# Dense attention stage: values as high and low part become the weights of the weighting, turned probabilities are streamed in two parts, the result is turned at the end

## The reference

```
def dense_block_attention(q, k, v):        # q: (B, L, Hkv, G, Dh); k, v: (B, L, Hkv, Dh)
    ...
        s = einsum('bqhgd,bkhd->bhgqk', qi, k) * scale      # scale = Dh ** -0.5
        p = softmax(s, axis=-1)
        return einsum('bhgqk,bkhd->bqhgd', p, v)
...
    qb = rms_norm(qb.reshape(b, l, B_KV_HEADS, g_b, HEAD_DIM), qn_b)
    kb = rms_norm(kb.reshape(b, l, B_KV_HEADS, HEAD_DIM), kn_b)
...
    ob = dense_block_attention(axial(qb), axial(kb), vb)    # axial: rotation of both halves of a head
```

## Time and profile before

| | us |
|---|---|
| median of 3 runs | 3950.07 |
| the profiled execution | 3949.25 |
| its span | 3947.4 |
| PE busy (matmul) | 3802.8 (96%) |
| PEld busy | 3570.8 (90%) |
| DVE busy | 2643.0 (67%) |
| ACT busy | 2096.3 (53%) |
| POOL busy | 854.5 (22%) |

### The profile page before, as it was taken

One profiled execution on the slowest core, in us unless ns is written; L12 is line 12 of the kernel. 1 busy time (PEld: TensorE's weight loads), 2 busy tenths in 40 slices (PEclk: granted clock), 3 DMA queues, 4 the chain that ended last, 5 costly groups with the idle time before them and its releaser, 6 DMA issues. The chain is left out here.

```text
span 3947.4 us, 70746 instructions
## 1 busy us (share of the span) xinstructions
PE 3802.8 (96%) x24950; PEld 3570.8 (90%) x24950; DVE 2643.0 (67%) x5354; ACT 2096.3 (53%) x3837; POOL 854.5 (22%) x1367
## 2 busy tenths in 40 slices
PE   8999999999999889999999999999997999999998
PEld 7989989999987789999999989999886999999998
DVE  6565664676665677777777757777536777777775
ACT  6544554555552255565556556555323556655654
POOL 5132230333330011121111133323000111111112
PEclk9999999999999999999999999999898999999999
DMA  3000001122124378887788731000335788778874
GB/s 110 10 22 7 24 17 36 45 69 64 49 97 154 130 248 248 264 256 241 243 266 255 242 91 47 31 24 16 137 139 192 234 251 271 246 238 252 270 245 134
DMA packets 492025, 583.96 MB, mean 148 GB/s; under 512 B 21536, under 2 KB 447520, under 8 KB 491808
## 3 DMA queue, kind: packets, MB, share of 16 engines
q1 hardware_dynamic: 473952, 522.44, 41.1%
q0 software_dynamic: 15680, 50.34, 5.4%
q10 hardware_dynamic: 2176, 8.39, 0.5%
HBM read 514.89 MB, written 66.22 MB: 147 GB/s over the span
## 5 line engine op out<-in xcount | busy, mean ns | idle before, releaser
L1774 DVE TENSOR_TENSOR wl<-raw,wh 128x2048 fp32r<-128x2048 f32 x384 | 876.1, 2289 | 193.6 <-ACT wh L1717 175.0
L1717 ACT CAST wh<-raw 128x2048 fp32r<-128x2048 f32 x384 | 730.5, 1910 | 24.4 <-DMA raw<-in_w_gate 22.1
L1890 PE MATMUL ps_g<-xT,wh 128*128 128x384 f32 x2048 | 594.2, 356 | 0.3 <-DVE xT L1780 0.3
L1890 PE MATMUL ps_u<-xT,wh 128*128 128x384 f32 x2048 | 593.5, 356 | 0.0
L1892 PE MATMUL ps_g<-xT,wl 128*128 128x192 f32 x2048 | 477.5, 254 | 0.0
L1892 PE MATMUL ps_u<-xT,wl 128*128 128x192 f32 x2048 | 477.3, 254 | 0.0
L151 PE MATMUL psP<-ring_high,hTh 128*128 128x384 f32 (+1 forms) x1344 | 459.8, 342 | 12.5 <-DVE ring_low L826 6.3
L153 PE MATMUL psP<-ring_high,hTl 128*128 128x384 f32 (+1 forms) x1344 | 441.3, 328 | 0.0
L152 PE MATMUL psP<-ring_low,hTh 128*128 128x384 f32 (+1 forms) x1344 | 440.9, 328 | 0.0
L1080 PEld LDWEIGHTS psO<-V,pT 128*128 128x128 f32 x3456 | 421.4, 194 | 20.3 <-issue 10.2
L1080 PE MATMUL psO<-V,pT 128*128 128x64 f32 x3456 | 419.5, 274 | 4.9 <-ACT pT L759 3.0
(11 more groups left out here) (219 smaller groups left out, 7715.4 us busy)
## 6 DMA issues: line engine op xcount, KB each, us to landing
raw<-in_w_gate SPq DMA_DIRECT2D x128, 1024.0 KB, 5.7
raw<-in_w_up SPq DMA_DIRECT2D x128, 1024.0 KB, 5.8
raw<-in_w_down SPq DMA_DIRECT2D x128, 1024.0 KB, 8.3
xb<-in_x SPq DMA_DIRECT2D x72, 256.0 KB, 2.8
out_y<-yb SPq DMA_DIRECT2D x24, 512.0 KB, 2.6
h_rows<-hb SPq DMA_DIRECT2D x24, 512.0 KB, 3.0
ring_raw<-in_w_a SPq DMA_DIRECT2D x24, 384.0 KB, 3.8
xb<-in_x SPq DMA_DIRECT2D x12, 512.0 KB, 4.6
```

The lines of the kernel that those rows point to most:

```text
L1717: act.copy(wh[:, j % SPL], raw[:, j % RAW]).then_inc(w_high, 1)
L1774: dve.tensor_tensor(wl[:, j % SPL], raw[:, j % RAW], wh[:, j % SPL].bitcast(F32), ALU.subtract)\
L1890: both = lambda **fl: pe.matmul(ps[:, f, 0:2 * CAP], wh[:, j % SPL, k, fs], xT[:, k].rearrange("p h c -> p (h c)"), **fl)
```

## The change

All of it is in the dense stage.

- The values are kept as a high part (fp32r) and a low part, side by side in `V` (128 columns). ACT writes them twice, once in float32 to `v32` and once rounded to `V`; POOL subtracts (the low part).
- Turned probabilities too: ACT copies both batches rounded (the high part), DVE subtracts from PSUM (the low part). `pT` has three places instead of two.
- For each block of keys one fp32r product: the weights are the 128 columns of `V`, and 256 columns are streamed, 128 of the high and 128 of the low part of the turned probabilities. In PSUM stand then four parts, turned around (features by queries): two halves of columns and two halves of rows.
- DVE adds the halves of columns (`join`, into `oT`), PE turns the sum (`turn_output`, event "O"), DVE adds the two other halves into `osb` (`add_halves`), and ACT divides (`divide`).
- The weighting of a unit is cut in two: its second batch comes after the transposes of the next unit. The list is R(n), V(n - 1, 1), S(n + 2), O(n - 1), V(n, 0).
- On DVE the maximum of unit n + 2 moves behind the additions of unit n - 1, and gives the negative maximum at once; the factor `SCALE` goes into the gains. The rotation's first product moves from DVE to POOL (four products per tile, into `xr`, after `squared`). In the unit after a projection `rotate` and `scale` now stand right behind the second subtraction (the event V(n - 1, 1) calls `tile_up_to(3)`), ahead of `add_halves` and of the maximum.
- To make room, x has three places instead of four, inside `qT`, and the rotation table holds each distinct part once, loaded by four transfers instead of one.

The diff, cut to its core:

```diff
@@ -351,12 +351,15 @@
                 events.append(("T", turned))
 
         for kind, n in plan:
+            if kind == "U" and n:
+                events += [("R", n), ("V", n - 1, 1)]
+            elif kind == "U":
+                events.append(("R", n))
             if kind == "P":
                 turn_up_to(n - 2)
...
                     since[p] += 1
-                events.append(("V", n))
+                if n:
+                    events.append(("O", n - 1))
+                events.append(("V", n, 0))
             else:
...
+    if dense:
+
+        x_places = [nc.alloc_sbuf_tensor_at(f"xb{x}_{state['n']}", [P, HC], F32, offset=qT_at + 4 * (x * TOK + TOK - HC))
+                    for x in range(XH)]
     kT = ph.sb("kT", [P, nkv, 2, TOK], F32R)
-    V = ph.sb("V", [P, NT, nkv * HD])
+    V = ph.sb("V", [P, NT, 2 * HD], F32R) if dense else ph.sb("V", [P, NT, nkv * HD])
     prob = ph.sb("prob", [P, 2, 2 * KC])
-    pT = ph.sb("pT", [P, 2, BLK * P]) if dense else ph.sb("pT", [P, nq // 2, 2 * KC])
+    if dense:
+        pT = ph.sb("pT", [P, SLOTS, BLK, 2, P], F32R)
+        v32 = ph.sb("v32", [P, 2, HD])
+        oT = ph.sb("oT", [P, 2, 2 * P])
+    else:
...
+                if dense:
+                    pool.tensor_tensor(V[:, t, HD:], v32[:, b, :], V[:, t, 0:HD].bitcast(F32), ALU.subtract).then_inc(v_split, 1)
                 for a in range(S1):
...
-                                                 spread(sn[:, c0:c0 + R1], 1, nh), ALU.mult)
+                        sn = rope[:, NT if a else t, (1 + f) * R1:(2 + f) * R1] if dense else rope[:, s, t, 1, c0:c0 + R1]
+                        ins = pool.tensor_tensor(qx[:, b, :, c0:c0 + R1], x[:, :, c1:c1 + R1], spread(sn, 1, nh), ALU.mult)
+                if dense:
+                    wait_alone(pool, squared, p + 1, tally)
+                    turned_x = xr[:, b, :].rearrange("p (h c) -> p h c", c=HD)
+                    for c0 in range(0, HD, R1):
+                        cs = rope[:, NT if c0 >= 2 * R1 else t, 0:R1]
+                        ins = pool.tensor_tensor(turned_x[:, :, c0:c0 + R1], x[:, :, c0:c0 + R1], spread(cs, 1, nh), ALU.mult)
                 ins.then_inc(crossed, 1)
                 wait_alone(pool, summed, p + 1, tally)
                 chain.link(pool.tensor_scalar(ms[:, b, :], ss[:, b, :], 1.0 / HD, em[:, steps[s]["order"], t:t + 1],
...
                 act.copy(xr[:, b, :], psP[:, 0:nh * HD])
-                act.mul(V[:, t, :], psP[:, nh * HD:NC], rt[:, steps[s]["order"], t:t + 1]).then_inc(evacuated, 1)
+                if dense:
+                    if p >= 2:
+                        act.wait_ge(v_split, p - 1)
+                    act.mul(v32[:, b, :], psP[:, nh * HD:NC], rt[:, 0, t:t + 1])
+                act.mul(V[:, t, 0:nkv * HD], psP[:, nh * HD:NC], rt[:, steps[s]["order"], t:t + 1]).then_inc(evacuated, 1)
 
             def square(p):
...
-                act.copy(pT[:, slot, at:at + w], room_of("R", u, k)[:, 0:w]).then_inc(pT_act, 1)
+                if dense:
+                    act.copy(pT[:, slot, :, 0, :], room_of("R", u, k).rearrange("p (x c) -> p x c", c=P)).then_inc(pT_act, 1)
+                else:
...
+            def divide(u):
+
+                segs = units[u][1]
+                act.wait_ge(rden_ready, u + 1)
+                act.wait_ge(o_added, u + 1)
+                for c, (h, t, *_) in enumerate(segs):
+                    out = osb[:, (units[u][0] * NT + t) % OR, h]
+                    ins = act.mul(out, out, rden[:, u % 4, c:c + 1])
+                ins.then_inc(o_done, 1)
 
...
+            def turned_low(u, k):
+                slot = work.spot(u, k)[0]
+                dve.wait_ge(pT_act, batch0[u] + k + 1)
+                dve.tensor_tensor(pT[:, slot, :, 1, :], room_of("R", u, k).rearrange("p (x c) -> p x c", c=P),
+                                  pT[:, slot, :, 0, :].bitcast(F32), ALU.subtract).then_inc(pT_dve, 1)
+
+            def join(u):
+
+                segs = units[u][1]
+                dve.wait_ge(pv_done, batch0[u] + 2)
...
+                for c in range(len(segs)):
+                    ins = dve.tensor_reduce(oT[:, u % 2, c * P:(c + 1) * P], o_half(u, c).rearrange("p (f c) -> p c f", f=2),
+                                            AX.X, ALU.add)
+                ins.then_inc(o_summed, 1)
+
+            def add_halves(u):
+
+                i, segs = units[u][0:2]
+                ns, (h, t) = len(segs), segs[0][0:2]
...
+                dve.wait_ge(exp_done, u + 1)
+                dve.reciprocal(rden[:, u % 4, 0:ns], den[:, u % 4, 0:ns]).then_inc(rden_ready, 1)
+                p = i * NT + t
+                if h == 0:
+                    for x in range(p, p + ns):
+                        if x >= OR:
...
+                dve.tensor_reduce(osb[:, p % OR:p % OR + ns, h],
+                                  room_of("O", u)[:, 0:ns * P].rearrange("p (n f c) -> p n c f", f=2, c=HD),
+                                  AX.X, ALU.add).then_inc(o_added, 1)
+
+            waiting = []
+
+            def maxima():
...
                     x_low_part(e[1], e[2])
-                if e[0] == "R":
+                if e[0] == "R" and dense:
+                    turned_low(e[1], 0)
+                    if e[1]:
+                        join(e[1] - 1)
+                    turned_low(e[1], 1)
+                    tile_up_to(1)
+                elif e[0] == "R":
                     copies(e[1])
-                    if dense:
-                        tile_up_to(1)
-                if e[0] == "S":
+                if e[0] == "S" and dense and e[1] > 1:
+                    waiting.append(e[1])
+                elif e[0] == "S":
                     if e[1] == 0:
                         mask_constants()
                     maximum(e[1])
-                    if dense:
-                        tile_up_to(2)
+                if e[0] == "O":
+                    if e[1] == UT - 1:
+                        join(e[1])
+                    add_halves(e[1])
+                    tile_up_to(2)
...
-                if e[0] == "V":
+                if e[0] == "V" and dense:
+                    maxima()
+                    tile_up_to(3)
+                elif e[0] == "V":
                     output(e[1])
-                    if dense:
-                        tile_up_to(3)
                 if e[0] == "OL":
...
 
+            def weigh_batch(u, k):
+                segs = units[u][1]
+                if k == 0:
+                    both = u > 0 and max(len(segs), len(units[u - 1][1])) > 1
+                    if u - 1 + both > 0:
+                        pe.wait_ge(o_summed, u - 1 + both)
+                    pe.wait_ge(v_split, units[u][3] + 1)
+                copied(u, k)
+                slot = work.spot(u, k)[0]
+                for x, (c, j) in enumerate(units[u][2][k]):
+                    k0, nk = segs[c][2:4]
+                    ins = pe.matmul(o_half(u, c), V[:, k0 + j, :], pT[:, slot, x, :, :].rearrange("p f c -> p (f c)"),
+                                    start=(j == 0), stop=(j == nk - 1))
+                ins.then_inc(pv_done, 1)
+
+            def turn_output(u):
+                pe.wait_ge(o_summed, u + 1)
+                room_free(("O", u))
+                for c in range(len(units[u][1])):
+                    ins = pe.transpose(room_of("O", u)[:, c * P:(c + 1) * P], oT[:, u % 2, c * P:(c + 1) * P], ident)
+                ins.then_inc(o_turned, 1)
+
             idle_bank = psS[:, 0, 0:P]
             if fresh[0]:
```

118 lines of the change are left out of this document (79 added, 39 removed).

## The result

The changed kernel takes 4052.66 us (median of 4 runs, 4049.59 to 4060.3) where the kernel before takes 3949.70: 103 us more, ratio 1.0267 with a 95% interval of 1.0255 to 1.0279. The direction was forecast, the size was not: 57 us were expected, and the time lies 8 us above the top of the range. The profiled execution of the changed kernel, the longest of its four, has a span of 4058.5 us, that of before 3947.4.

A forecast was written before the change was run, and what follows sets the result against it. TensorE bounds the unit before; after, three engines share one tight loop (2.87, 3.00, 3.04 us). Terms -48 + 56 + 9 + 19 + 11 + 9 + 1.4 = +57.4 on 3950.07 give 4007.5 us, range 3940 to 4045.

The forecast's parts named there:

- The unit: Sample units of the dense stage: 3.04 us each instead of 3.54, over 96 units -48 us.
- rival D: Much slower: the sum of halves runs at half rate, 0.35 us a unit more; 4041 us, chance 0.12.
- Rival B: Faster: TensorE stays the bound, waits at tiles covered but for 1 us; 3917 us, chance 0.15.
- A projection between units: Twelve places where a projection stands between units: 9.03 us over three units against 4.38, +56 us.
- (1): After the projection ScalarE empties PSUM before copying probabilities: first copy at +1.47 instead of +0.65, subtraction at +2.11.
- (2): VectorE's rotation and scaling, waiting for GpSimd, precede sum and maximum: a step of 6.3 us where a unit has 3.04.
- step (3): Next unit's second transposes wait for that sum, then weighting, scores, tile's turn and low parts follow: a step of 4.55.
- The stretches: Stretches of projections: GpSimd's longer chain at two pairs of tiles a turn, 3 us in each of three turns, +9.
- The start: Start of the dense stage: three places for x and GpSimd's 6.4 us a tile against 5.6, +9 us together.
- Passages and quarters: Four places where a stretch passes into units, +19 us; low parts of ten weight quarters no longer hidden, +11 us.
- What was to show it: Signs: maximum every 3.0 to 3.1 us, 18 us over three steps, VectorE idle over 2 us a tile, stage past 700.
- C: Even: units gain 64 us as with TensorE the bound, but 3 us are lost per tile; 3949 us, chance 0.12.

The follow-up runs named there:

- e4: Changed kernel with one of GpSimd's four cosine products a tile, the other three left out; 4011.61 us.
- f1: Changed kernel with all of a tile's cosine products on VectorE (two instructions) instead of GpSimd (four); 4012.91 us.
- f3: Changed kernel with later rotation and scaling, a later turn for tiles between units, and cosine products on VectorE; 3991.05 us.
- g1: Changed kernel with that later order, cosine products on GpSimd for tiles projected between units and on VectorE for the others; 3977.38 us.

## Why the prediction was wrong

**The unit: right.** 3.05 us against 3.04 forecast; prompt units 3.53 against 3.5. The two subtractions take 685 ns, the sum of halves 415 ns: the row of 416 ns with plain order was the right one to take, and rival D, the sum at half rate, is out. The other units gained 22.7 us where 30 less 2 for the quarters stood, 28: eight of the 62 steps are prompt units, which gained nothing. Rival B, TensorE stays the bound, is out too: TensorE is idle 153 of 776 us. The judgement by the share of weight loads, for which the prediction named the Trainium skill, "Perfetto Trace Analysis", Identifying the Most-Contended Engine, pointed to TensorE before; the changed trace shows what it can't see, that the engine with 407 of 672 us was next and had its slack in the wrong places.

**A projection between units: the mechanism right, 24 us too little.** Steps (1), (2) and (3) gave 18.15 us for three steps; with the clock held up they are 18.22, in the changed kernel 19.6 to 20.4 (20.7 to 21.1 at the first place of a turn). What failed is that step (3) was worked out with durations of a TensorE at 2.4 GHz, behind a wait of its own making. The second long step is 4.5 us at 1.00 and 5.7 to 6.4 with the clock down: 19.5 us over 12 places. In the earlier trace rows the clock is 1.00, and TensorE's longest idle stretch between two products of that stage is 1.9 us; a forecast that makes it idle has to ask what the next products then cost. The other 5 us are mostly the first places of three turns, where the first step is 11.9 us instead of 10.7: it holds the sums of a prompt unit and two weight quarters that the prediction's ten don't include.

**The stretches: mis-sized, +9 against +31.8.** The prediction counted GpSimd's longer chain for two pairs of tiles in a turn's stretch, 1.5 us each. Timeline of the changed kernel in one:

```profile
436.36 0.32 ACT L760 ACTIVATE V<-psP,roots 128x64 fp32r<-128x64 f32 x1
...
437.77 0.32 POOL L694 TENSOR_TENSOR V<-v,V 128x64 fp32r<-128x64 f32 x1
...
439.17 1.16 POOL L705 TENSOR_TENSOR xr<-xg,rope 128x64 f32<-128x64 f32 x4
440.37 0.43 DVE L921 TENSOR_TENSOR xg<-xr,qx 128x256 f32<-128x256 f32 x1 [2.78 <-POOL xr L705]
...
442.11 0.82 DVE L929 TENSOR_TENSOR xn<-xg,rstd 128x192 f32<-128x192 f32 x1 [1.31 <-POOL rstd L710]
442.85 0.34 DVE L933 TENSOR_SCALAR xn<-xg,rstd 128x128 f32<-128x128 f32 x1
...
443.24 0.44 PE L1161 MATMUL psT<-ident,xn 128*128 128x128 f32 x2 [2.73 <-DVE xn L933]
```

From the values' end (436.68) it is 6.5 us to the scaling's end, just ahead of the tile's turn at 443.24, where the sum had 5.9. Most of the difference is L929: 0.82 us here, while GpSimd runs the next tile's gain, and 0.36 at 357.71 above, where GpSimd is idle. In this trace it is 0.82 to 0.84 at all nine tiles where it overlaps that gain, three a stretch, and 0.36 at the 39 others; the gain itself takes no longer. No run tests the cause. So the chain's length was nearly right, and the count was too low. How often a stretch waits for the chain no run tells cleanly. With 0.85 us less a tile (e4) a stretch was 5.9 us shorter, but in that run L929 is never slow, which may be 1.4 us of it, and the clock doesn't fall, which may be 2.3. The rest, 2.2 to 5.9 us, is the chain at three to seven tiles, where the prediction had two. Of the 31.8 us, 18.5 go with the cosine products (f1), slow L929 and lost clock among them, 6.7 more with the order (f3), and 6.6 stay, 2.2 a stretch, at a clock of 1.00; of these no run tells the second value product from the rest.

**The start: mis-sized, +9 against +16.5.** The same chain: 11.2 us go with the cosine products, and some 3.5 is the places for x in one profile. The term had 6.4 instead of 5.6 us from tile to tile; measured are 6.8 to 6.9 instead of 5.5, so 1.3 us a tile where it had 0.8.

**Passages and quarters: 12 us too much.** The prediction gave the four passages 19 us for their projections and 9 for eight of the ten quarters, 28 in all; they cost 15.5, lost clock included. That is luck in the total: without it the forecast would have been further off.

**What was to show it.** A maximum every 3.05 us: yes. VectorE idle over 2 us a tile at rotation and scaling: 2.1. The dense stage beyond 700 us: yes. 18 us over three steps: no, 20, and that was the sign of the clock.

Rivals B and C had waits covered but for 1 to 3 us a tile, and the order of the changed kernel doesn't cover them. The order is no necessity, though: with it mended the gain of the units comes through at most steps, and with the cosine products moved back as well 75 of the 103 us go away. No version tried beats the kernel before. The remainder of 29 us lies more in the passages (+16.5 in g1) than between units; whether the tile's work can be taken off VectorE, or the clock held up in the passages, was not tried.

## What to carry to other kernels

When an edit makes the second engine nearly as full as the first, price not only the loop but each instruction that was free beside it: waits ahead of the loop's own work, and then the work itself, come back at full length. Where a forecast leaves TensorE idle for some us, its next products may run at half speed; a few useless products in the gap tell whether they do. And before work is moved to a "quiet" engine (GpSimd had 175 of 672 us), follow the chain it stands in: its share of busy time says nothing about who waits for its last result.

## What the runs showed of the hardware

In the changed kernel TensorE's clock fell to 0.50 at all 12 places between units, where the engine waits 2.9 to 3.2 us, and stayed there for some 3 to 7 us. With waits of 2.1 us (e4) it still fell at 11 of the 12. In the kernel before, whose longest idle stretch between two products of the stage is 1.9 us, it never fell. Ten products of the identity (20 records, 2.4 us busy a place) held it at 1.00 over 80 us (300 to 380), and at 12 places won 16 us of time. Moving a tile's cosine products from VectorE (one instruction of 0.42 us) to GpSimd (four, 1.15 us) cost 36 us in the kernel before, 0.75 us a tile over 48 tiles, on an engine busy 26% of the stage. And VectorE's scaling (L929) took 0.82 us instead of 0.36 wherever GpSimd's gain ran beside it, at nine of 48 tiles.
